# Latent values one item behind, swapped keys copied inside the projection, banded gates on GpSimd

## The reference, cut to what matters

```python
# latent (layers 0 and 3)
p = softmax(q @ k.T * scale)            # token queries see 768 keys, context queries 256
y = ((p @ v) * silu(gate)) @ w_out
# banded (layer 1)
s_ctx  = q @ k_c.T * scale
s_band = where(mask, q @ k_band.T * scale, -1e30)
o_x = softmax_with_sink([s_ctx, s_band], sink) @ [v_c, v_band]
y_x = (o_x * silu(gate_x)) @ w_out
y_c = (softmax_with_sink([q_c @ k_c.T * scale], sink) @ v_c * silu(gate_c)) @ w_out
```

## Time and profile before

| what | us |
|---|---|
| median of three runs | 3804.34 (3803.0 to 3804.67) |
| profiled execution, device time | 3801.59 |
| profiled execution, span in the trace | 3799.9 |
| attention stage of latent layer 0 | 205.6 (1553.4 to 1759) |
| attention stage of latent layer 3 | 165 (3563 to 3728) |
| banded layer, first score product to last gate | 186 (2115.4 to 2301.5) |

### The profile page before, as it was taken

The page is one execution under the profiler, slowest core; times in us unless marked ns, Lnnn a source line. Parts: engine busy times, 40 slices in busy tenths (PEclk is TensorE's granted clock), DMA queues, the critical chain, the costliest instruction groups (busy, mean ns, idle before and its releaser), DMA issues. The chain is left out here.

```text
span 3799.9 us, 35661 instructions
## 1 busy us (share of the span) xinstructions
PE 3135.8 (83%) x13906; PEld 1853.6 (49%) x13906; DVE 1140.4 (30%) x2404; ACT 738.8 (19%) x1627; POOL 238.0 (6%) x274
## 2 busy tenths in 40 slices
PE   7999965778785798888899789899867783888888
PEld 3458633444442655654455454455533242464564
DVE  3441620000000101233210583333038685301232
ACT  2112710000000212332201462100011110212331
POOL 0000001000001000000000000011104251000000
PEclk9999976888888899999999999999978786999999
DMA  6664327999998011100011200122230104011100
GB/s 225 233 223 141 115 74 258 365 366 361 367 359 303 19 44 42 59 1 23 11 34 44 79 1 1 42 94 82 71 127 6 34 31 166 15 42 55 64 1 22
DMA packets 247217, 437.02 MB, mean 115 GB/s; under 512 B 27769, under 2 KB 108169, under 8 KB 247084
## 3 DMA queue, kind: packets, MB, share of 16 engines
q1 hardware_dynamic: 233868, 401.61, 30.4%
q0 software_dynamic: 8096, 25.19, 2.0%
q10 hardware_dynamic: 5120, 8.39, 0.6%
HBM read 401.85 MB, written 32.52 MB: 114 GB/s over the span
## 5 line engine op out<-in xcount | busy, mean ns | idle before, releaser
L1881 PE MATMUL moe_ph<-moe_w,moe_x_T 128*64 128x256 f32 x2048 | 272.0, 425 | 143.8 <-DMA moe_w<-w 123.8
L299 PE MATMUL hyena_in_main<-hT,second_weights 128*128 128x256 f32 (+1 forms) x1024 | 330.5, 486 | 1.4 <-PEq L765 1.4
L1881 PEld LDWEIGHTS moe_ph<-moe_w,moe_x_T 128*64 128x64 f32 x2048 | 160.8, 154 | 258.3 <-issue 182.1
L299 PEld LDWEIGHTS hyena_in_main<-hT,second_weights 128*128 128x128 f32 x1024 | 194.5, 190 | 137.2 <-issue 124.0
L299 PE MATMUL swa_in_main<-hT,second_weights 128*128 128x512 f32 (+1 forms) x576 | 189.4, 489 | 6.7 <-DMA second_weights<-b_w_in 5.3
L1177 PE MATMUL qkv_main<-hT,first_weights 128*128 128x512 f32 (+1 forms) x384 | 167.8, 580 | 0.9 <-PEq L765 0.9
L299 PEld LDWEIGHTS swa_in_main<-hT,second_weights 128*128 128x128 f32 x576 | 109.9, 191 | 86.6 <-issue 73.8
L1994 DVE TENSOR_TENSOR moe_act_rows<-moe_ph,moe_act 128x256 f32<-128x256 f32 x32 | 13.6, 425 | 435.1 <-PE moe_ph L1881 435.1
L533 PE MATMUL mla_att_o_bank<-mla_att_probs_T,hT 128*128 128x128 f32 x832 | 102.6, 279 | 33.4 <-ACT mla_att_probs_T L671 33.4
L589 DVE TENSOR_REDUCE mla_att_maxes<-mla_att_scores 128x1 f32<-128x768 f32 (+1 forms) x80 | 64.4, 846 | 213.0 <-PE mla_att_scores L504 213.0
L1903 PE MATMUL moe_py<-moe_w,moe_act_T 128*64 128x512 f32 x512 | 116.9, 598 | 2.1 <-ACT moe_act_T L1975 2.1
(11 more groups left out here) (427 smaller groups left out, 4920.3 us busy)
## 6 DMA issues: line engine op xcount, KB each, us to landing
moe_w<-w SPq DMA_DIRECT2D x96, 2048.0 KB, 16.6
first_w_out<-w_mod SPq DMA_DIRECT2D x12, 2048.0 KB
mixT<-w_mod SPq DMA_DIRECT2D x12, 2048.0 KB, 8.1
first_weights<-w_in SPq DMA_DIRECT2D x16, 1024.0 KB
second_weights<-c_w_in SPq DMA_DIRECT2D x16, 1024.0 KB
second_weights<-b_w_in SPq DMA_DIRECT2D x10, 1024.0 KB
scr_expert_rows<-moe_y ACTq DMA_DIRECT2D x64, 128.0 KB, 6.3
second_weights<-a_w_in SPq DMA_DIRECT2D x7, 1024.0 KB
```

The costliest lines, as they stand in the source:

```text
L299: mm = pe.matmul(main[u][0:unit.rows, 0:unit.cols], lhsT, rhs, start=(c == 0), stop=(c == r.kc - 1))
L1881: mm = pe.matmul(bank[half * T:(half + 1) * T, 0:HF], x_T[s][:, c, :], w[s][:, c, half * HF:(half + 1) * HF], start=(c == 0), stop=(c == K ...
```

## The change

Three edits, all in the second block.

1. In the not-deep order TensorE now goes `scores(k+1)`, `turn(k)`, `values(k-1)`, with `values` of the last item behind the loop; `gate_out` on VectorE moves one item back with it. Only the two latent layers use that order.
2. `project` takes a list `copies`. For the banded layer GpSimd issues four DMAs there (the two halves of `other_k`, the mask, the sinks) once the five groups of the first range are done, and waits for them inside the projection stage. The `once` list and its two waits are gone from `pair_attend`.
3. The banded items have no gate. ScalarE's `copy_out` takes the result out of PSUM, and GpSimd multiplies by the gates in place, one instruction of 128 x 768 for each of the 8 head pairs, when the six items of the pair are out.

```diff
-def project(nc, name, ranges, consts, ahead=None):
+def project(nc, name, ranges, consts, ahead=None, copies=()):
...
+                if copies:
+
+                    for u, _ in ranges[0].indices(0):
+                        pool.wait_ge(s_out[u], ranges[0].groups)
+                    for dst, src in copies:
+                        pool.dma_start(dst, src).then_inc(s_copies, 16)
+                    pool.wait_ge(s_copies, 16 * len(copies))
...
-                for dst, src in once:
-                    sp.dma_start(dst, src).then_inc(s_once, 16)
...
-                if once:
-                    pe.wait_ge(s_once, 16 * len(once))
...
                         turn(k)
-                        values(k)
+                        if k:
+                            values(k - 1)
+                    values(N - 1)
...
-                if once:
-                    dve.wait_ge(s_once, 16 * len(once))
...
-                        if gated:
-                            gate_out(k)
+                        if k and gated:
+                            gate_out(k - 1)
+                    if gated:
+                        gate_out(N - 1)
...
                 st.clear_last_pool(pool)
+                for upto, tile, gate in gates:
+
+                    pool.wait_ge(s_out, upto)
+                    nc.gpsimd.tensor_tensor(tile, tile, gate, ALU.mult)
...
+    gates=[((p + 1) * (XT + CT), hT[:, p, :], gate[:, p, :]) for p in range(B_HEADS // 2)])
```

More of the change, by code:

```diff
@@ L244, in project @@
         s_out = st.sems("out_ready", n_units)
+        s_copies = st.sem("first_range_copied")
         s_stored, stored0 = st.stored_sems([16 * n for n in sent])
@@ L415, in pair_attend @@
 def pair_attend(nc, name, items, consts, slots, scale=1.0, region_banks=1, loads=(), ring=1, w_out=None,
-                w_out_after=None, once=(), probs=None):
+                w_out_after=None, probs=None, gates=()):
     with Stage(nc, name) as st:
@@ L435, in pair_attend @@
         MX, NEG, SUM, BELOW, SINK, ALL, INV = range(7)
-        s_once = st.sem("once_in")
         s_load = st.sems("bias_in", ring)
@@ L2243, in swa @@
         other_k, mask, sink = sb("other_k", [P, n_k, TOK]), sb("band", [P, CTX + 3 * P]), sb("sinks", [P, B_HEADS])
+        k = qk[:, n_q:n_q + n_k, :]
         project(nc, "swa_in", [
@@ L2247, in swa @@
             Range(B_WIDTH // GROUP, columns(w_in, B_WIDTH + 2 * B_KVW, KD), kept_features(gate, "silu", True), hT, KD)],
-            consts, ahead=ahead)
-        k = qk[:, n_q:n_q + n_k, :]
-        once = [(mask[:], a["swa_mask"]), (sink[:], a["b_sink"].to_broadcast([P, B_HEADS])),
-                (other_k[HD:P, :, :], k[0:HD, :, :]), (other_k[0:HD, :, :], k[HD:P, :, :])]
+            consts, ahead=ahead,
+            copies=[(other_k[HD:P, :, :], k[0:HD, :, :]), (other_k[0:HD, :, :], k[HD:P, :, :]), (mask[:], a["swa_mask"]),
+                    (sink[:], a["b_sink"].to_broadcast([P, B_HEADS]))])
         items = []
@@ L2273, in swa @@
                         [piece(0, X, TOK), piece(CTX, lo * P, (hi + 1) * P)], values([XT, XT + 1] + list(range(lo, hi + 1))),
-                        hT[:, p, qs], bias=[[mask[:, 0:CTX]] * 2, [mask[:, at:at + n]] * 2], sink=sinks,
-                        gate=gate[:, p, qs]))
-                else:
-                    items.append(PairItem([piece(0, X, TOK)], values([XT, XT + 1]), hT[:, p, qs], sink=sinks,
-                                          gate=gate[:, p, qs]))
-        pair_attend(nc, "swa_att", items, consts, 3, scale=HD ** -0.5, w_out=a["b_w_out"][0], once=once)
+                        hT[:, p, qs], bias=[[mask[:, 0:CTX]] * 2, [mask[:, at:at + n]] * 2], sink=sinks))
+                else:
+                    items.append(PairItem([piece(0, X, TOK)], values([XT, XT + 1]), hT[:, p, qs], sink=sinks))
+        pair_attend(nc, "swa_att", items, consts, 3, scale=HD ** -0.5, w_out=a["b_w_out"][0],
+                    gates=[((p + 1) * (XT + CT), hT[:, p, :], gate[:, p, :]) for p in range(B_HEADS // 2)])
     post(hT[:])
```

## The result

The changed kernel takes **3760.11 us** (median of 4 runs, 3757.75 to 3763.48) where the kernel before, on the same chip, takes 3803.67 (3802.67 to 3804.67): a ratio of 0.9886, 95% interval 0.9869 to 0.9903, 43.6 us saved. The prediction was 3761 us, range 3752 to 3777. The profiled execution took 3761.22 us with a span of 3759.5.

A forecast was written before the change was run, and what follows sets the result against it. TensorE, busy 83% of the span, was taken as the bound. Savings of 11.0 + 11.1 + 11.5 + 9.2 = 42.8 us took the profiled 3801.59 to 3758.8; with 2.75 for the median, 3761 us, range 3752 to 3777.

The forecast's parts named there:

- Layer 3: Latent layer 3: values one item behind no longer wait for ScalarE's copy of the transposed probabilities; 11.0 us saved.
- slack to `exp`: Latent layer 3: scores could start at 4.81 us, while `exp` releases their region at 4.47; 0.34 us to spare.
- rival (b): Latent layers: TensorE's clock falls in idle of about 2.5 us, 2.7 us at about five places; 13 more, 3774; chance 0.08.
- Layer 0: Latent layer 0: values one item behind save 2.65 us per pair of heads, about 0.5 back; 11.1 us saved.
- Edit 2: Banded stage start: no wait for `other_k`, 13.0 us saved, less 1.5 for sharing the weight load; net 11.5, bounds 8 and 13.
- Edit 3: Banded gates: 13.3 us saved at seven changes of pair, less 2.1 turn-taking and 2.0 tail; net 9.2, bounds 0 and 15.
- the turn-taking: Banded layer: GpSimd's products hold up VectorE at the shared SBUF ports; 0.3 us a pair, 2.1 in all.
- The tail: Banded stage's end: the eighth GpSimd product, behind the last copy and ahead of the barrier, adds 2.0 us with its wait.
- Rival (c): Banded layer turn-taking costs the full 1.5 us a pair and shared loads 3 us; 10 more, 3771; chance 0.14.
- rival (d): Banded stage: GpSimd and VectorE block each other, about 7 us per gate product; slower than before; chance 0.02.
- rival (a): Latent layers: `exp` becomes the bound, releasing 0.4 us later than counted; 11 us less gain, 3772; chance 0.12.
- Rival (e): Projection stage: copies are late and it ends later, the wait merely moving; 12.4 us more, 3773; chance 0.03.

The follow-up runs named there:

- without products: The changed kernel with GpSimd's eight banded gate products left out, so the banded layer has no gates: 3753.9 us.
- the fastest kernel: The changed kernel with banded gates on VectorE two items behind, needless products in the latent layers' waits, and key copies issued past the weight load: 3737.2 us, ratio 0.9820.
- edit 3 alone: The kernel before with only the banded gates moved to GpSimd, multiplied once a pair of heads: 3798.7 us, ratio 0.9980.
- edit 1 alone: The kernel before with only the latent layers' values and gates issued one item behind: 3779.7 us, ratio 0.9928.
- the kernel with two products: The changed kernel with each of GpSimd's eight banded gate products issued twice, first into a spare tile: 3778.5 us.

## Why the prediction was right, step by step

**Layer 3, 11.0 predicted, 12.0 measured**, from two errors that nearly cancel. The period of an item is 8.78 us where I had 8.98. In the sum I put the ends of rows where the next row's start was needed: successive pieces of TensorE's work overlap by 0.17 us, so the values start 1.89 us after the first transpose instead of 2.06. The slack to `exp` that I put at 0.34 is then 0.11, and it held. Over 13 items that is 2.5 us more. Against it, rival (b) came true at the layer's first item: the clock fell behind the wait of 2.45 us, the products there took 4.54 us, and the first item grew by 0.7 us where I had it shrink by 1.05. The end cost 1.3 us where the sum had 1.5, with the two sets of values last:

```profile
3682.34 5.52 PE L538 MATMUL mla_att_o_bank<-mla_att_probs_T,hT 128*128 128x128 f32 x48
```

**Layer 0, 11.1 predicted, 10.3 measured.** The same two errors, with more of the second. t0 and t5 wait for `exp` as walked through, 2.45 us at the first item and 2.55 at t5, but only 1.56 at the t0 of later pairs. But the sum took 2.85 us for the scores after the 1.60 us wait from the earlier trace rows. That row was one of three: the same wait was followed by 4.54 us in the third and fourth pair of heads of the kernel before. This is the third pair's:

```profile
1661.69 4.54 PE L504 MATMUL mla_att_scores<-mla_kn,mla_qn 128*128 128x512 f32 x8 [1.60 <-ACT second_weights L664]
```

After 2.55 us it is 4.5 each time. Rival (b) was thus the case, and its price was wrong: 1.5 to 1.8 us at each of five places, not 2.7, and two of the five were slow before. Besides, the scores after the 4.03 us wait, which is in both kernels, took 4.53 us in the one profile and 5.49 in the other. By the five sets the fall cost the changed kernel 8.3 us, some 3.4 of which the kernel before had paid too. It did not end at 3774, as the rival had it, since the shorter items paid for it.

**Edit 2, 13.0 less 1.5 predicted; 12.6 less 0.6 measured in the changed kernel, less 1.1 on average of seven profiles.** The first banded product starts 0.05 us after SyncE's first issue at 2092.32. The 1.5 was a guess between 0 and 3 that came near. Its working does not hold: the earlier trace rows have 203 GB/s at a DMA share of 0.62, which leaves 0.12 MB/us in the other 0.38 and not 0.38 MB/us, and 1.1 MB would take 9 us at that rate. No wait grew by 3 us or more.

**Edit 3, 9.2 predicted, 8.8 measured.** The pair was to take 22.92 - 1.9 + 0.3 = 21.3 us and takes 21.37, with luck: both terms were put too small, by about the same. VectorE's freedom gives 2.1 to 2.2 a pair (20.8 without products) and the turn-taking takes 0.6. The tail cost 1.9, near the 2.0 of the sum. Rival (c), 1.5 us a pair, did not come; rival (d) needed 7 us a product and the rows show 1.81 with at most 0.6 of it on the path. Of rival (a) the slack of 0.11 shows how near it was. Rival (e) did not come.

**The sum.** 42.8 us predicted; 43.7 in the three stages, and 3.3 back elsewhere in the profiled execution. Of these 0.6 are the longer wait for weights, which belongs to edit 2; for the other 2.7 no edit can be named. The rest of the program takes 3229.7 us in the kernel before and 3224.8 to 3233.9 in the eleven others: the fastest kernel has the shortest rest, edit 3 alone the longest, and its stages outside are the same instructions. By the medians the change gave 43.6. The prediction was near because its errors were of both signs, which is luck; the waits that it said would close did close, and the ones that it said would open opened.

## What to carry to other kernels

Issuing a product one item behind pays only up to the next thing that the loop waits for; walk the whole loop, by starts and not by ends, and ask what late release comes next. Where the order leaves TensorE idle for a couple of microseconds once per group, look at how long the first work behind the gap takes, at every occurrence and not one: a few needless products in the gap can win it back, if they are no longer than the gap. Before moving elementwise work from VectorE to GpSimd, try it later on VectorE: here the work cost 0.1 us a pair (with the copies out gone in exchange), the waiting 2.1, and GpSimd 0.6 a pair for its turn at SBUF and 1.9 at the end. Before putting a price on a shared transfer, read the same wait in every trace that has it: one profile said 0.6 us, seven say 0.6 to 1.9.

## What the runs showed of the hardware

- TensorE's granted clock fell from 1.00 to 0.50 (1.2 GHz) behind waits as short as 2.07 us (in four of seven pairs of the kernel with two products) and 1.60 us (five of nine times in the three kernels with the old latent order), and in the latent layers behind each unfilled wait of 2.45 us or more. Behind the 1.56 us waits of the new order it never fell, 18 times in six profiles, so the length of a wait alone does not tell. A group of eight score products took 2.75 to 2.85 us at full clock, 4.30 to 4.54 behind most falls, 5.49 at worst. Behind a filled wait it never fell.
- A filler product (128x128 by 128x128, two records each in the trace) took 0.24 us; ten of them in a wait of 2.5 us left 0.2 to 0.3 us of it.
- A VectorE step on 128x2 elements with both inputs in SBUF took 0.81 us beside one GpSimd product and 1.73 us between two, instead of 0.16, and ended with the product each time.
- 1.1 MB of copies issued beside a 1 MB load of weights made TensorE's wait for that load 5.78 to 7.08 us in seven profiles, against 5.05 to 5.43 in the five without.
- Stages outside the edits vary: the rest of the program took 3229.7 us before, 3231.4 with edit 1 alone and 3233.9 with edit 3 alone, which change nothing in it, and 3224.8 to 3233.9 over all twelve profiles. A stage that is not touched came out alike to 0.1 or 0.2 us where the clock was the same.
